# The convolution's layer norm: GpSimd adds the four channel blocks, TensorE sums one block

## What is computed

```
u = val * sigmoid(glu)
u = depthwise_conv(u, 31 taps) + bias              # each of 512 channels by itself
u = silu(layer_norm(u)) * silu(cgate)              # mean and variance over the 512 channels
y = u @ w_o
```

## Time and profile before

| what | value |
|---|---|
| median of the runs | 1273.69 us (1272.31 to 1273.85) |
| profiled execution, its own time | 1272.52 us |
| its span | 1271.2 us |
| mean granted TensorE clock | 0.983 of full speed |
| TensorE matmuls busy | 1216.9 us, 96% of the span |
| VectorE busy | 899.7 us, 71% |
| ScalarE busy | 583.3 us, 46% |
| GpSimd busy | 260.8 us, 21%, 215 instructions |

### The profile page before, as it was taken

The page is one execution under the profiler, slowest core; times in us unless marked ns, Lnnn a source line. Parts: engine busy times, 40 slices in busy tenths (PEclk is TensorE's granted clock), DMA queues, the critical chain, the costliest instruction groups (busy, mean ns, idle before and its releaser), DMA issues.

```text
span 1271.2 us, 19629 instructions
## 1 busy us (share of the span) xinstructions
PE 1216.9 (96%) x7720; PEld 998.8 (79%) x7720; DVE 899.7 (71%) x1704; ACT 583.3 (46%) x975; POOL 260.8 (21%) x215
## 2 busy tenths in 40 slices
PE   6999988999998999997999999999999999899998
PEld 5877867778777778885777778888898767689997
DVE  4897776787887444599999663336776797876665
ACT  3455532455555543332444344324563663346553
POOL 0200103110233312441000031222451131201223
PEclk9999998999999999998999999999999998999999
DMA  7874576463634311222222222334653232225453
GB/s 255 287 263 159 193 275 214 166 220 109 236 117 157 101 51 51 67 67 83 67 67 67 67 67 85 97 100 125 208 161 108 73 112 84 84 86 152 142 155 116
DMA packets 49133, 168.11 MB, mean 132 GB/s; under 512 B 5841, under 2 KB 7057, under 8 KB 48785
## 3 DMA queue, kind: packets, MB, share of 16 engines
q1 hardware_dynamic: 49041, 166.86, 39.6%
HBM read 165.79 MB, written 1.05 MB: 131 GB/s over the span
## 4 chain that ended last, share of the span: by engine, by line
PE 77%; DVE 15%; issue 4%; POOL 1%; ACT 1%; DMA 0%; SPq 0%; DVEq 0%; ACTq 0%; POOLq 0%
PE bank L1586 9%; PE bank L1604 9%; PE bank L1588 8%; PE bank L1587 8%; PE bank L1606 8%; PE bank L1605 8%; PE bank L1513 4%; DVE w_lo L2390 3%; PE bank L1628 3%; PE bank L1630 3%; PE bank L1629 3%; DVE conv_val L2723 2%; PE bank L1905 2%; PE bank L1931 2%; PE bank L1698 1%
## 5 line engine op out<-in xcount | busy, mean ns | idle before, releaser
L2390 DVE TENSOR_TENSOR w_lo<-w_raw,w_hi 128x1024 fp32r<-128x1024 f32 (+3 forms) x264 | 322.5, 1226 | 166.9 <-ACT w_hi L1970 165.7
L1970 ACT ACTIVATE w_hi<-w_raw 128x1024 fp32r<-128x1024 f32 (+3 forms) x264 | 269.7, 1026 | 335.2 <-issue 112.7
L1586 PE MATMUL bank<-w_hi,x_hi 128*128 128x512 f32 (+4 forms) x736 | 294.8, 401 | 4.8 <-DVE w_lo L2390 4.0
L1588 PE MATMUL bank<-w_hi,x_lo 128*128 128x512 f32 (+4 forms) x736 | 279.1, 379 | 0.0
L1587 PE MATMUL bank<-w_lo,x_hi 128*128 128x512 f32 (+4 forms) x736 | 279.0, 379 | 0.0
L1604 PE MATMUL bank<-x_hi,w_hi 128*128 128x512 f32 (+1 forms) x640 | 225.5, 352 | 1.1 <-ACT merged L2212 0.8
L1606 PE MATMUL bank<-x_lo,w_hi 128*128 128x512 f32 (+1 forms) x640 | 216.4, 338 | 0.0
L1605 PE MATMUL bank<-x_hi,w_lo 128*128 128x512 f32 (+1 forms) x640 | 216.2, 338 | 0.0
L1586 PEld LDWEIGHTS bank<-w_hi,x_hi 128*128 128x128 f32 x736 | 140.2, 190 | 36.9 <-issue 7.8
L1588 PEld LDWEIGHTS bank<-w_hi,x_lo 128*128 128x128 f32 x736 | 139.7, 190 | 26.3
L1587 PEld LDWEIGHTS bank<-w_lo,x_hi 128*128 128x128 f32 x736 | 140.0, 190 | 22.5
(11 more groups left out here) (355 smaller groups left out, 1764.3 us busy)
## 6 DMA issues: line engine op xcount, KB each, us to landing
w_raw<-in_w SPq DMA_DIRECT2D x172, 512.0 KB, 3.5
w_raw<-in_wm SPq DMA_DIRECT2D x48, 512.0 KB, 5.3
w_raw<-in_wo SPq DMA_DIRECT2D x40, 512.0 KB, 4.2
w_raw<-in_wy_gla SPq DMA_DIRECT2D x8, 512.0 KB, 3.5
w_raw<-in_wy_att SPq DMA_DIRECT2D x8, 512.0 KB, 3.5
w_raw<-in_wy_conv SPq DMA_DIRECT2D x8, 512.0 KB, 3.6
w_raw<-in_w SPq DMA_DIRECT2D x8, 460.0 KB, 4.7
w_raw<-in_w SPq DMA_DIRECT2D x12, 288.0 KB, 2.8
```

Source lines behind the costliest of these rows:

```text
L1586: mm(out, xh[:, q, col], hi[:, kk, 0:w], start=kp == 0 and kk == 0 and not with_bias, stop=False)
L1588: ins = mm(out, xl[:, q, col], hi[:, kk, 0:w], start=False, stop=last and kk == KP - 1)
L1970: do(hi, raw, ACT.Copy).then_inc(sem["cut_hi"], 1)
L2390: v.tensor_tensor(lo, raw, hi.bitcast(F32), ALU.subtract).then_inc(sem["cut_lo"], 1)
```

## The change

`conv_mean` and `conv_var` issue one matmul each in place of four. Its operand is the sum of the four blocks, and that sum is made by GpSimd: three additions of whole blocks for the values (`conv_add`, j = 1 to 3) ahead of the mean, and three for the squares (`conv_add2`, j = 1 to 3) ahead of the variance. In each layer GpSimd has six instructions more, of 128 x 512 in layer 0 and 128 x 256 in layer 1, and TensorE six matmuls fewer. The sum of the values stands in block 0 of the tile of squares (`u2`), so that in layer 0 the first `conv_add` waits for the last `y2_gate`, as `conv_sq` did before; with it the mean waits, which did not wait for it. The sum of the squares is made in place in the same block. The planner gets the new steps at 1.2 us each, and 0.9 us in place of 3.4 us for `conv_mean`; `conv_var` stays at 1.89 us.

```diff
 def conv_end(l):
-    yield [("conv_mean", l)]
+    yield [("conv_add", l, j) for j in range(1, 4)] + [("conv_mean", l)]
     for j in range(4):
-        yield [("conv_dev", l, j), ("conv_sq", l, j)]
+        yield [("conv_dev", l, j), ("conv_sq", l, j)] + ([("conv_add2", l, j)] if j > 0 else [])
...
-    "POOL": "roped sub_sq sub_pow ln_pow ln_pool mean_w mi_pow mi_add u_zero conv_u conv_g acc_add y2_gate gla_zero "
+    "POOL": "conv_add conv_add2 roped sub_sq sub_pow ln_pow ln_pool mean_w mi_pow mi_add u_zero conv_u conv_g acc_add y2_gate gla_zero "
...
-    "conv_mean": lambda l: [("mean_w",), ("tap", l, TAPS - 1, 3)],
+    "conv_add": lambda l, j: [("tap", l, TAPS - 1, 0), ("tap", l, TAPS - 1, j), ("conv_add", l, j - 1), ("gla_o", 0, 1)] + (
+        [("y2_gate", l, 3)] if l == 0 else []),
+    "conv_add2": lambda l, j: [("conv_sq", l, 0), ("conv_sq", l, j), ("conv_add2", l, j - 1)],
+    "conv_mean": lambda l: [("mean_w",), ("conv_add", l, 3)],
...
-    "conv_var": lambda l: [("conv_sq", l, 3)],
+    "conv_var": lambda l: [("conv_add2", l, 3)],
...
-        pe.wait_ge("tap", l, TAPS - 1, 3)
+        pe.wait_ge("conv_add", l, 3)
         pe.wait_ge(*(before or ()))
-        for j in range(4):
-            ins = mm(k.bank[i][:, 0:n_tok], b.mean_w[:, :], b.cv[:, j, 0:n_tok], start=j == 0, stop=j == 3)
-        ins.then_inc(sem["conv_mean"], 1)
+        mm(k.bank[i][:, 0:n_tok], b.mean_w[:, :], b.u2[l][:, 0, 0:n_tok], start=True, stop=True).then_inc(sem["conv_mean"], 1)
...
-        pe.wait_ge("conv_sq", l, 3)
+        pe.wait_ge("conv_add2", l, 3)
         pe.wait_ge(*(before or ()))
-        for j in range(4):
-            ins = mm(k.bank[i][:, 0:n_tok], b.mean_w[:, :], b.u2[l][:, j, 0:n_tok], start=j == 0, stop=j == 3)
-        ins.then_inc(sem["conv_var"], 1)
+        mm(k.bank[i][:, 0:n_tok], b.mean_w[:, :], b.u2[l][:, 0, 0:n_tok], start=True, stop=True).then_inc(sem["conv_var"], 1)
...
+    def conv_add(l, j):
+        n_tok = len(tiles_of(l)) * P
+        total = b.u2[l][:, 0, 0:n_tok]
+        pool.wait_ge("tap", l, TAPS - 1, j)
+        if j == 1:
+            pool.wait_ge("tap", l, TAPS - 1, 0)
+            if l == 0:
+                pool.wait_ge("gla_o", l, 1)
+                pool.wait_ge("y2_gate", l, 3)
+            part = b.cv[:, 0, 0:n_tok]
+        else:
+            pool.wait_ge("conv_add", l, j - 1)
+            part = total
+        g.tensor_tensor(total, part, b.cv[:, j, 0:n_tok], ALU.add).then_inc(sem["conv_add"], 1)
+
+    def conv_add2(l, j):
+        n_tok = len(tiles_of(l)) * P
+        total = b.u2[l][:, 0, 0:n_tok]
+        pool.wait_ge("conv_sq", l, j)
+        if j == 1:
+            pool.wait_ge("conv_sq", l, 0)
+        else:
+            pool.wait_ge("conv_add2", l, j - 1)
+        g.tensor_tensor(total, total, b.u2[l][:, j, 0:n_tok], ALU.add).then_inc(sem["conv_add2"], 1)
```

More of the change, by code:

```diff
@@ L752 @@
     "att_t_act": 0.4, "att_t_dve": 0.35, "att_v": 0.5, "bias0": 4.5, "bias1": 4.5, "bias_sel": 1.4, "bias_zero": 1.1,
[L753 to L770, removed]
+    "conv_add": 1.2, "conv_add2": 1.2, "conv_dev": 0.6, "conv_g": 1.25, "conv_hi": 0.33, "conv_lo": 0.79, "conv_mean": 0.9,
@@ new lines @@
+    "conv_n": 0.6, "conv_rs": 2.56, "conv_sd": 0.5, "conv_silu": 0.75, "conv_sq": 0.52, "conv_u": 1.25, "conv_var": 1.89,
+    "conv_ve": 0.6, "cut_hi": 1.0, "cut_lo": 1.2, "ev1": 0.48, "ev2": 0.48, "ev_ag": 0.54, "ev_cg": 0.57, "ev_fv": 0.4,
+    "ev_gate": 0.73, "ev_glu": 0.57, "ev_sig": 0.48, "ev_val": 0.57, "ev_y": 0.5, "flip": 0.32, "flip_hi": 0.36,
+    "flip_hi y1": 0.58, "flip_lo": 0.6, "fox_c": 0.6, "fox_cols": 0.35, "fox_cum": 0.1, "fox_e": 2.0, "fox_l": 0.1, "fox_z": 0.2,
+    "gate_diag": 0.2, "gate_mul": 0.49, "gate_ones": 0.25, "gate_rows": 0.48, "gate_silu": 0.45, "gated": 1.0, "gla_a": 0.86,
@@ new lines @@
+    "gla_con": 0.6, "gla_cp": 1.85, "gla_cum": 0.93, "gla_dec": 0.14, "gla_e": 2.6, "gla_e12": 1.0, "gla_e3": 0.55,
+    "gla_iv": 2.3, "gla_kf": 0.3, "gla_ki": 1.25, "gla_ks": 1.25, "gla_kt": 0.6, "gla_la": 0.6, "gla_left": 0.93, "gla_m": 0.6,
+    "gla_ms": 0.52, "gla_o": 3.6, "gla_o1": 0.3, "gla_o2": 0.33, "gla_one": 0.54, "gla_qf": 0.43, "gla_qi": 0.89, "gla_qt": 0.48,
+    "gla_sq": 1.25, "gla_st": 0.55, "gla_tot": 0.9, "gla_z": 1.0, "gla_zero": 2.2, "heads": 0.43, "heads iq": 0.55,
+    "heads_act": 0.48, "heads_dve": 0.6, "hr_add": 1.25, "hr_add q": 3.39, "hr_iv": 1.58, "hr_ms": 0.6, "hr_n": 1.8,
@@ new lines @@
+    "hr_sq": 0.59, "index_iw": 0.1, "index_relu": 0.45, "index_sel": 0.14, "index_top": 0.6, "index_w": 0.5, "lam": 0.4,
+    "lam_dots": 0.74, "lam_exp": 0.2, "ln_dve": 1.3, "ln_pool": 3.24, "ln_pow": 1.74, "ln_stat": 0.25, "ln_x": 0.75, "load": 2.0,
+    "lr_flip": 0.43, "lr_t": 0.48, "m_hi": 0.58, "m_lo": 0.6, "mean_w": 0.2, "mi_act": 0.98, "mi_add": 1.0, "mi_dve": 0.79,
+    "mi_flip": 0.3, "mi_hi": 0.55, "mi_lo": 0.78, "mi_ms": 0.1, "mi_pow": 0.71, "mi_sq": 1.1, "mi_x": 1.04, "mod": 0.25,
@@ L772 @@
+    "mod_col": 0.1, "mod_row": 0.2, "mod_t": 0.25, "out_add": 1.25, "out_gate": 0.6, "project_y y0": 1.05, "resid": 1.36,
+    "rope": 1.3, "roped": 2.34, "scale": 0.55, "sub_end": 0.8, "sub_pow": 2.3, "sub_sq": 1.25, "sub_sum": 0.79, "tap": 0.66,
+    "u_zero": 1.95, "y2_gate": 1.25, "y2_hi": 0.55, "y2_lo": 0.6}
 TABLE = {"lam_exp": "exp", "att_exp": "exp", "gla_e3": "exp", "gla_dec": "exp", "gla_e12": "exp", "a_exp": "exp",
@@ L1026 @@
 SPARE = 64
-SHARED = {"project": "projected", "project_t": "projected", "project_y": "projected", "mod": "projected",
+SHARED = {"conv_add": "conv_u", "conv_add2": "conv_g", "project": "projected", "project_t": "projected", "project_y": "projected", "mod": "projected",
           "att_s": "scored", "a_s": "scored", "att_max": "max_found", "a_max": "max_found",
@@ L3147, in out_add @@
         g.tensor_tensor(dst, dst, b.gtmp[:, i, :], ALU.add).then_inc(sem["out_add"], 1)
-    pool.run({"roped": roped, "sub_sq": sub_sq, "sub_pow": sub_pow, "ln_pow": ln_pow,
+    pool.run({"conv_add": conv_add, "conv_add2": conv_add2, "roped": roped, "sub_sq": sub_sq, "sub_pow": sub_pow, "ln_pow": ln_pow,
               "ln_pool": ln_pool, "mean_w": mean_w, "mi_pow": mi_pow,
```

## The result

The changed kernel takes 1278.9 us (median of five runs, 1276.8 to 1280.16), the kernel before 1273.85 in the runs beside it. The ratio is 1.0043 with a 95% interval of 1.0032 to 1.0053: slower by about 5 us, where 1269.3 was forecast and 1275.5 was the upper end of the range. The profiled execution is the shortest of the five (1276.8 us); its span is 1275.5 us, the span before was 1271.2.

A forecast was written before the change was run, and what follows sets the result against it. TensorE, busy 96% of the span, was taken as the bound, with VectorE where TensorE waits for it. -7.76 + 2.9 + 0 + 0.5 = -4.4 us gave a median of 1269.3; range for 8 of 10: 1265.3 to 1275.5.

The forecast's parts named there:

- The terms of the matmuls: Both layers' sums: one matmul for four saves 5.16 us in layer 0 and 2.60 in layer 1, together 7.76.
- the 0.5 us put down for the additions: Layer 1, last taps to variance: six GpSimd additions mostly fall into VectorE's gaps, cost 0.5 us, bounds 0 and 4.4.
- The attention moves up: Layer 0 from 704 us: without the mean, attention steps start sooner, so all 2.58 us of the first sum is gained.
- The stall ahead of y2, 2.9 us: Layer 0 at 739.6 us: three additions hold VectorE's `gate_diag` and `y_lo`, so y2 begins 2.9 us later, bounds 0 and 4.7.
- `y_lo`, whose stretching was a sign of being right: Layer 0 behind `y2_gate`: `gate_diag` and `y_lo` were to be stretched, TensorE idling about 3 us ahead of y2.
- The `conv_add2` of layer 0 at nothing: Layer 0 ahead of the variance: three additions of squares, 3.87 us on GpSimd, cost nothing; at most 3.87.
- stays covered: Layer 1's norm ahead of y0: chain 0.3 us longer, slack shrinks from 4.0 us to about 1.1, no wait.
- counted a redrawn order only around 704 us in layer 0: Layer 0, 704 to 733 us: a changed order of attention steps leaving TensorE idle was named as a sign of error.
- if it is not, y0 waits by what is missing: Layer 1's y0: fallback should the norm's slack not cover it; no size given.
- a wait for `conv_lo` ahead of y0: Layer 1: sign of error, TensorE waiting for the norm's `conv_lo` before y0; no size given.
- The stall lowers the clock: Rival, layer 0 near 740 us: TensorE's wait lowers its clock, up to 3.4 us lost, at most 1272.7 us; chance 0.12.
- GpSimd's time becomes TensorE's: Rival, both layers: every addition holds VectorE its whole length, 12.1 us against 7.76, +4.4, 1278.0 us; chance 0.13.

The follow-up runs named there:

- early_len34: after_len34 with layer 0's sum of values in another tile, so that `conv_add` doesn't wait for `y2_gate`: 1267.34 us, ratio 0.9947.
- layer1_len34: Kernel before with the additions and single matmuls in layer 1 alone, `conv_mean` planned at 3.4 us: 1270.76 us, ratio 0.9981.
- after_len34: Changed kernel with the planner's old length for `conv_mean` put back, 3.4 us in place of 0.9: 1271.2 us, ratio 0.9977.
- layer0_only: Kernel before with the change in layer 0 alone; `conv_mean` planned at 0.9 us there, 3.4 in layer 1: 1273.65 us, ratio 1.0002.
- sd_first: Changed kernel with one planner edge keeping layer 1's square root (`conv_sd`) ahead of `ev_cg`: 1277.99 us, ratio 1.0026.
- length_only: Kernel before with only the planner's length for `conv_mean` changed, 0.9 us in place of 3.4; no additions: 1281.38 us, ratio 1.0056.
- sd_first_again: The same kernel as sd_first, run once more on another stretch of the chip: 1274.07 us, ratio 1.0011.
- before_sd_late: Kernel before with one planner edge putting layer 1's square root (`conv_sd`) behind the four `ev_cg`: 1282.56 us, ratio 1.0068.

## Why the prediction was wrong

- **The terms of the matmuls were right.** A sum has two records where eight were, 0.88 us at 750.51 in place of 3.44; and where nothing stands in the way, both stages move up by at least the sum: 5.2 in layer 0 (early_len34, forecast 5.16), 2.8 in layer 1 (layer1_len34, 2.60), where the 0.5 us put down for the additions shows in the last tap and not on TensorE.
- **"The attention moves up" was right**: the step that releases `gate_diag` came 4.2 us sooner, 3.5 without the first column's 0.8. That is the whole 3.44 of the mean, since the mean itself moved behind y2.
- **The stall ahead of y2, 2.9 us, was right in place and mechanism and a little too large:** from 0.59 to 2.62 in the chain, 2.0 us. The place from which it followed is the row of `gate_diag` beside `y2_gate`. The forecast held three VectorE instructions for an addition each; only two `gate_diag` were held (1.29 us each), the third ran between two additions (0.27), and `y_lo`, whose stretching was a sign of being right, kept its time.
- **The `conv_add2` of layer 0 at nothing was wrong, by 1.9 us.** `conv_dev` and `ev_y` kept their time as said (0.687 and 0.684 us beside `acc_add`). But four more `gate_diag`, which the prediction didn't place there, met the three `conv_add2` at 755.95 us, and TensorE idled 0.64 and 0.69 us for them (the row of 2.33 us in the chain above). From y2's first matmul to its second half it is 38.25 us, before 38.04, though 3.44 - 2 x 0.86 = 1.72 of matmuls left this stretch: 1.9 in all. With it the stage adds up: -5.16 + 2.0 + 1.9 = -1.3, measured -1.2. In after_len34 one of the two waits is left (0.69 us), and the stage gains 1.9; in early_len34, where `conv_add2` comes at 744.47, both are gone.
- **The step that failed: layer 1's norm "stays covered", with 4.0 us of slack shrinking to 1.1.** The slack was read from an order of ScalarE that the change didn't keep. A smaller number for `conv_mean` in the planner's table was enough to put the root behind `ev_cg`, and the root came 9.8 us after its operand (before: at once). The prediction knew that order is planned, and counted a redrawn order only around 704 us in layer 0, not in the queue of the engine to which the change gives nothing. Its sentence "if it is not, y0 waits by what is missing" and its sign of error, a wait for `conv_lo` ahead of y0, are what happened, with no price in the sum: 6.1 us of waits and 1.6 of lowered clock. For layer 1's stage -2.1 us was forecast and +4.6 measured; for layer 0's, -2.3 and -1.2.
- **The rivals.** "The stall lowers the clock" came in some executions and not in others (1.6 us in layer0_only and sd_first, nothing in the kernel after). "GpSimd's time becomes TensorE's" gave nearly the measured time (1278.0), but by luck: its mechanism did not make the loss in layer 1, where after_len34 and layer1_len34 have the same additions and gain 3.3 us from the last tap on.
- **The Trainium skill** (GPSIMD Engine Reference, "Key points") was followed for `conv_dev`, and the trace bears it out as far as it goes: the one `conv_dev` beside `acc_add` took 0.687 us, the last, whose end lies beside the first `conv_add2`, 0.675; before, with GpSimd idle, 0.681. On ScalarE, the Trainium skill (ScalarE: Activation LUTs, "What ACT_TABLE_LOAD costs") gives about 1283 ns for a table load plus a drain of some 1380 ns at each switch. The load agrees (1.28 us in every row). No drain beside it is seen here: the root starts 0.02 us after its load ended (1165.72 + 1.28 = 1167.00, 1167.02). Two more loads are thus 2.6 us of ScalarE; the 7.7 us lost at y0 are more than that, so the order in which they stand costs more than they do.

## What to carry to other kernels

Where a planner draws the order, its assumed lengths are part of the kernel: change the instructions and keep the lengths first (after_len34), change the lengths alone too (length_only), and compare the order of every engine, also of those to which the edit gives nothing. A slack read from a trace holds only for the order of that trace. And an addition on GpSimd is cheap or dear by its neighbours on VectorE: layer 0's additions cost 2.0 + 1.9 us beside `gate_diag`, and nothing where they come earlier.

## What the runs showed of the hardware that was not expected

- VectorE and GpSimd hold each other up, both ways. `gate_diag` (128 x 128) takes 0.28 us alone, up to 1.325 beside `y2_gate` and 1.30 beside an addition, about as long as the GpSimd instruction. A weight cut beside `acc_add` lost 1.0 us as well (2.23 at 752.01, in place of 1.23). `ev_y`, with a PSUM operand, lost nothing. And `y_lo`, when it started first (735.35 and 738.57 us in the kernel after), kept its 0.68 us, while the additions that began beside it took 1.64 and 1.68 us in place of 1.27.
- The same wait of TensorE lowers its clock in one execution and not in the next: behind the stall at 740 us it is 1.00 in the kernel after and in sd_first_again, 0.84 and 0.82 in layer0_only. At 1045 to 1060 us all kernels wait for the same 3.15 us, and the clock behind it differs; windows of the kernel after, to the earlier trace rows:

```profile
1045.00:1050.00 5.00, 1.37 (x7) 1.17 (x8) 5.00 (x10) 2.23 (x4) 2.18 (x1) 0.75 0.36 105
1050.00:1055.00 5.00, 5.00 (x17) 4.28 (x17) 4.86 (x8) 1.69 (x3) 1.40 (x1) 0.50 0.22 80
1055.00:1060.00 5.00, 5.00 (x34) 5.00 (x33) 2.68 (x4) 3.02 (x5) 2.33 (x2) 0.73 0.07 28
```

Followed matmul by matmul from the start of y2's second half, the kernel after falls 0.6 us behind the kernel before at 1045 to 1060 us and 0.5 more behind a second wait at 1105 to 1118; with the 0.5 of the last tap this is the table's third column. Neither the order nor the shift decides it: layer0_only and sd_first have the orders of the kernel after on every engine up to 1137 us and reach y2's second half at 782.55 and 782.23 us, but stand at -0.4 and +2.6. What decides how the clock falls was not settled.
- Executions differ by up to 3.5 us before 704 us with equal orders on all engines (-0.8 in the kernel after, +2.7 in before_sd_late); what starts them on one course or the other was not settled either.
